# One pair of column blocks per feed-forward layer as seven block products in place of eight (Strassen's scheme)

## The reference

```python
def swiglu(x, w_gate, w_up, w_down):
    return (jax.nn.silu(x @ w_gate) * (x @ w_up)) @ w_down      # x 256x1024, w 1024x2816 and 2816x1024
```

## Time and profile before

| | |
|---|---|
| median of three runs | 1620.4 us (1619.58 to 1620.77) |
| profiled execution, span from first to last instruction | 1618.1 us |
| the median over that span | 2.3 us |
| TensorE matmul records | 7791 |
| weight and other data moved | 306.8 MB, mean 190 GB/s |

### The profile page before, as it was taken

How to read it: one execution, slowest core, us unless ns; L and a number is a source line. 1 busy time by engine, 2 the same in 40 slices (tenths; PEclk the granted TensorE clock), 3 DMA queues, 4 the chain that set the end, 5 groups by cost and what they waited for, 6 DMA issues and landing times.

```text
span 1618.1 us, 18458 instructions
## 1 busy us (share of the span) xinstructions
PE 1609.3 (99%) x7791; PEld 1342.0 (83%) x7791; DVE 957.4 (59%) x959; ACT 776.3 (48%) x815; POOL 78.7 (5%) x104
## 2 busy tenths in 40 slices
PE   9999999999999999999999999999999999999998
PEld 7888897788888888888988888888888998888886
DVE  6555466676554775455668545565446657685553
ACT  7444447655443764442656434354443436454340
POOL 0121000000000000001010000000000131000000
PEclk9999999999999999999999999999999999999999
DMA  9856474466654866563647546666555554576560
GB/s 319 231 179 208 157 240 140 163 198 219 192 187 131 276 205 185 159 221 98 237 158 253 182 156 211 204 201 188 161 206 182 196 178 148 182 241 188 162 216 26
DMA packets 222097, 306.77 MB, mean 190 GB/s; under 512 B 8896, under 2 KB 144320, under 8 KB 221888
## 3 DMA queue, kind: packets, MB, share of 16 engines
q1 hardware_dynamic: 217232, 290.29, 55.4%
q0 software_dynamic: 4416, 15.05, 2.9%
q10 hardware_dynamic: 368, 0.27, 0.1%
HBM read 304.52 MB, written 1.05 MB: 189 GB/s over the span
## 4 chain that ended last, share of the span: by engine, by line
PE 99%; DVE 0%; DMA 0%; SPq 0%; ACT 0%; issue 0%; DVEq 0%
PE bank L696 29%; PE bank L709 29%; PE bank L700 26%; PE bank L646 3%; PE bank L713 3%; PE bank L773 2%; PE bank L775 2%; PE bank L776 2%; PE bank L1117 0%; PE bank L907 0%; DMA raw<-in_ffn_w_up 0%; PE bank L926 0%; PE bank L916 0%; PE bank L1054 0%; PE bank L759 0%; PE bank L1136 0%
## 5 line engine op out<-in xcount | busy, mean ns | idle before, releaser
L1614 DVE TENSOR_TENSOR low<-raw,hiw 128x2048 fp32r<-128x2048 f32 (+2 forms) x296 | 631.4, 2143 | 382.9 <-ACT hiw L1229 381.9
L1229 ACT ACTIVATE hiw<-raw 128x2048 fp32r<-128x2048 f32 (+1 forms) x280 | 521.8, 1871 | 358.1 <-DMA raw<-in_ffn_w_out 87.9
L696 PE MATMUL bank<-hiw,xh 128*128 128x512 f32 x1404 | 384.9, 396 | 0.0
L709 PE MATMUL bank<-low,xh 128*128 128x512 f32 x1404 | 376.3, 390 | 0.0
L700 PE MATMUL bank<-hiw,xl 128*128 128x512 f32 x1232 | 330.1, 390 | 0.0
L709 PEld LDWEIGHTS bank<-low,xh 128*128 128x128 f32 x1404 | 263.2, 188 | 55.8 <-DVE low L1614 0.2
L696 PEld LDWEIGHTS bank<-hiw,xh 128*128 128x128 f32 x1404 | 257.1, 188 | 52.5 <-issue 2.8
L700 PEld LDWEIGHTS bank<-hiw,xl 128*128 128x128 f32 x1232 | 231.2, 188 | 49.6
L696 PE MATMUL bank<-hiw,th 128*128 128x512 f32 x524 | 143.7, 392 | 0.0
L700 PE MATMUL bank<-hiw,tl 128*128 128x512 f32 x524 | 142.2, 389 | 0.0
L709 PE MATMUL bank<-low,th 128*128 128x512 f32 x524 | 142.1, 389 | 0.0
(11 more groups left out here) (276 smaller groups left out, 1177.9 us busy)
## 6 DMA issues: line engine op xcount, KB each, us to landing
raw<-in_ffn_w_in SPq DMA_DIRECT2D x176, 512.0 KB, 4.9
raw<-in_ffn_w_out SPq DMA_DIRECT2D x40, 1024.0 KB, 5.0
raw<-in_ret_w_in SPq DMA_DIRECT2D x24, 1024.0 KB, 5.1
raw<-in_ffn_w_gate SPq DMA_DIRECT2D x42, 512.0 KB, 4.3
raw<-in_ffn_w_up SPq DMA_DIRECT2D x42, 512.0 KB, 5.3
raw<-in_ffn_w_down SPq DMA_DIRECT2D x20, 1024.0 KB, 5.1
raw<-in_w_in SPq DMA_DIRECT2D x16, 1024.0 KB, 5.7
raw<-in_gla_w_in SPq DMA_DIRECT2D x12, 1024.0 KB, 5.2
```

Source lines behind the costliest of these rows:

```text
L696: pe.matmul(o[:, :], tokens(0, k), whi[:, k, :], start=start and k == 0, stop=False, skip_group_check=True)
L709: ins = pe.matmul(o[:, :], tokens(0, k), wlo[:, k, :], start=False, stop=end, skip_group_check=True)
L1229: act.activation(hiw[s][:, 0:n], raw[s][:, 0:n], ACT.Copy).then_inc(hi.mark(i), 1)
L1614: dve.tensor_tensor(low[s][:, c0:c1], raw[s][:, c0:c1], hiw[s][:, c0:c1].bitcast(F32), ALU.subtract).then_inc(lo.mark(*what), 1)
```

## The change

In each feed-forward layer blocks 3 and 4 are computed together. With x11, x12 the first 128 tokens over rows 0 to 511 and 512 to 1023, x21, x22 the other 128, b11, b21 the weights of block 3 and b12, b22 those of block 4 for the same halves of the rows, the seven products are b11, t1, t2, b22, t3, b21, t4 (named by their weight operand): t1 = b12 - b11, t2 = b22 - t1, t4 = b21 - t2, t3 = b22 - b12. The token operands are x11, s0, s1, s3, s2, x12, x22 with s0 = x21 + x22, s1 = s0 - x11, s2 = x11 - x21, s3 = x12 - s1. Each product is one pass of 12 matmuls, alternately into banks 6 and 7, which the gate and up products didn't use. All sums are made in fp32 on DVE, and their results are split into high and low parts like any tile. Between the products stand whole tiles of the blocks 5 to 8, and the turns of the pair come later than in order:

```diff
+LOAD_LEAD, HIGH_LEAD = 6, 4
+FFN_PAIRS = (3,)
+FFN_STEPS = (
+    ("tile", 0, 0), ("tile", 0, 1), ("tile", 1, 0), ("tile", 1, 1), ("turn", 0),
+    ("token sums",),
+    ("tile", 2, 0), ("tile", 2, 1), ("turn", 1), ("blocks",),
+    ("product", 0, "b11"), ("tile", 5, 0),
+    ("product", 0, "t1"), ("tile", 5, 1), ("turn", 2),
+    ("product", 0, "t2"), ("tile", 6, 0),
+    ("product", 0, "b22"), ("tile", 6, 1), ("turn", 5), ("p",),
+    ("product", 0, "t3"), ("tile", 7, 0), ("turn", 4),
+    ("product", 0, "b21"), ("tile", 7, 1), ("turn", 6),
+    ("product", 0, "t4"), ("tile", 8, 0), ("tile", 8, 1), ("turn", 3), ("turn", 7),
+    ("tile", 9, 0), ("tile", 9, 1), ("turn", 8),
+    ("tile", 10, 0), ("tile", 10, 1), ("turn", 9))
```

PE's part, with what each product waits for:

```diff
+        def pe_product(pe, i, xh_of, xl_of, o, start):
+            whi, wlo = weight(i)
+            pe_hi(pe, i)
+            for k in range(4):
+                pe.matmul(o[:, :], xh_of(k), whi[:, k, :], start=start and k == 0, stop=False, skip_group_check=True)
...
+                elif m == "t1":
...
+                        pe.wait_ge(fn.sem, fn.of("sh", name))
+                        pe.wait_ge(vec.sem, vec.of("sl", name))
...
+                    pe_product(pe, grp[g].t1, *s_block(f, 0), bank[7], True)
+                elif m == "t2":
+                    pe.wait_ge(fn.sem, fn.of("u1", name, g))
+                    pe_product(pe, grp[g].t2, *s_block(f, 1), bank[6], False)
+                elif m == "b22":
+                    pe.wait_ge(fn.sem, fn.of("s5", name, g))
+                    pe_product(pe, grp[g].b22, *s_block(f, 3), bank[7], False)
+                elif m == "t3":
+                    pe.wait_ge(fn.sem, fn.of("u2", name, g))
+                    pe_product(pe, grp[g].t3, *s_block(f, 2), bank[6], False)
+                elif m == "b21":
+                    pe.wait_ge(vec.sem, vec.of("c12", name, g))
+                    pe_product(pe, grp[g].b21, *x_block(0, 1), bank[7], True)
+                else:
+                    pe.wait_ge(vec.sem, vec.of("c22", name, g))
+                    pe_product(pe, grp[g].t4, *x_block(1, 1), bank[6], False)
```

ACT copies the running sums u1, s5 and u2 out of PSUM, into memory of `xn` that is free meanwhile, and takes silu of the finished ones. DVE makes the weight sums in front of the lows, the token sums, and adds the copies to later products:

```diff
+        def dve_weight_sums(dve, i):
...
+            if m == "b11":
+                freed(dve, load_after[g.t1])
+                loaded(g.b11)
+                loaded(g.t3)
+                dve_sum(dve, g.t1, g.t3, g.b11)
...
+            elif m == "b22":
+                dve_sum(dve, g.t3, g.b22, g.t3)
...
+            dve.tensor_tensor(xs, xh[:, :, :].bitcast(F32), xl[:, :, :].bitcast(F32), ALU.add).then_inc(
+                vec.mark("xs", name), 1)
...
+            dve.tensor_tensor(sx[:, 0, :, :], a21, a22, ALU.add).then_inc(vec.mark("s", name, 0), 1)
...
+                if m == "b22":
+                    added(g, grp[g].b22, "u2", u2, bank[7], "c12")
+                    times(u2[:, 256:512], u2[:, 256:512], u2[:, 0:256], second, 0)
+                elif m == "t3":
+                    added(g, grp[g].t3, "s5", s5, bank[6], "c22")
+                    times(s5[:, 256:512], s5[:, 256:512], s5[:, 0:256], second, 1)
```

Weight memory is now given in single blocks of 128 x 2048, 14 at most (12 in f1 and f2), one for the raw and low part and one for the high part of a tile, each to the oldest, along an order of loads, highs and sums. The high part can wait for another tile than the load, so ACT has a wait of its own for it:

```diff
+            for i in range(first, end):
+                if tiles[i].pieces:
+                    events.append((load_key[i] - LOAD_LEAD, "load", i))
+                events.append((i - HIGH_LEAD, "high", i))
...
+                        load_key[grp.t3], load_key[grp.b22], load_key[grp.b21] = (
+                            grp.b11 + 0.5, grp.t1 - 0.1, grp.t2 - 0.1)
...
-            while j + 1 < NT and j < i + 5 and freed_by[j + 1] <= i - 2:
+            while j + 1 < NT and j < i + 5 and needed[j + 1] <= i - 2:
```

More of the change, by code:

```diff
@@ L98 @@
 Weight = namedtuple("Weight", "pieces k width")
-Ffn = namedtuple("Ffn", "name nx turned_raw th tl sg hh")
+Ffn = namedtuple("Ffn", "name nx turned_raw th tl sx sh sl sg hh")
+Group = namedtuple("Group", "first second b11 t1 t2 b22 t3 b21 t4")
 Edge = namedtuple("Edge", "n nx kind gains scale final early mid late")
@@ L235, in build @@
             rvl1 = sb("rvl1", [P, 2048], F32R, ar)
[L236 to L239, removed]
+        weight_block()
+        weight_block()
         U = []
@@ L387, in build @@
[L387 to L395, removed]
@@ L816, in pe_ffn @@
                 turn(0)
[L817 to L829, removed]
-                if j:
-                    turn(j - 1)
+                steps = FFN_STEPS[LEAD_STEPS:]
+            for step, *what in steps:
+                if step == "tile":
+                    tile(*what)
+                elif step == "turn":
+                    turn(*what)
+                elif step == "product":
+                    product(*what)
             T = (f.th, f.tl)
@@ L1588, in act_program @@
             act.wait_ge(tile_1.sem, tile_1.of("first"))
[L1589 removed]
+            act.activation(split[high_to[1]][:, 0:1024], whole[load_to[1]][:, 0:1024], ACT.Copy).then_inc(hi.mark(1, "first"), 1)
             act_turn_in(act, 0, 1)
@@ L1843, in dve_ffn @@
                 turn(0)
-            for j in range(0 if name == "f1" else 2, 11):
-                dve_lows(dve, 4 if name == "f1" and j == 0 else ahead(gu[2 * j + 1]))
-                mult(j, 0)
-                mult(j, 1)
-                if j:
-                    turn(j - 1)
-                if name == "f2" and j == 4:
+                steps = FFN_STEPS[LEAD_STEPS:]
+            for step, *what in steps:
+                if step == "tile":
+                    j, n = what
+                    if name == "f1" and j == 0:
+                        dve_lows(dve, 4)
+                    else:
+                        dve_lows(dve, ahead(spot[name, j, n]))
+                    if n:
+                        mult(j, 0)
+                        mult(j, 1)
+                elif step == "turn":
+                    turn(*what)
+                elif step == "token sums":
+                    dve_token_sums(dve, f)
+                elif step == "blocks":
+                    dve.wait_ge(fn.sem, fn.of("sh", name))
+                    dve.tensor_tensor(f.sl[:, :, :, :], f.sx[:, :, :, :], f.sh[:, :, :, :].bitcast(F32),
+                                      ALU.subtract).then_inc(vec.mark("sl", name), 1)
+                elif step == "product":
+                    dve_lows(dve, ahead(spot[(name, *what)]))
+                    product(*what)
+                elif step == "p" and name == "f2":
                     dve.wait_ge(fn.sem, fn.of("ph"))
```

382 lines of the change are left out of this document (291 added, 91 removed).

## The result

The changed kernel takes 1622.37 us (median of 20 runs, 1621.38 to 1624.62). The kernel before took 1620.24 us beside it (20 runs, 1619.58 to 1621.07). The ratio is 1.0014, 95% interval 1.0008 to 1.0021. So nothing was gained: the time rose by 2.1 us, which is within 0.2% of no change. The forecast was 1608.0 us, with a range of 1603.6 to 1616.0, and the time lies outside it.

A forecast was written before the change was run, and what follows sets the result against it. PE was taken as the bound, 99% of the chain. 16.3 - 4 x 0.9 - 0.3 = 12.4 us off the 1618.1 span gives 1605.7; with the median 2.3 above, 1608.0 us, range 1603.6 to 1616.0.

The forecast's parts named there:

- The price removed: PE, six feed-forward layers: 72 matmuls fewer of 7791, 2.72 us a layer, 16.3 us in all.
- The ledger of a0: Layer a0, turn of block 1 to turn of block 4: DVE needs 40.0 us, so PE waits 0.9 us.
- the four layers named: a0, a1, b0, b1: each waits 0.9 us at block 4's turn; f1 and f2 were forecast not to wait.
- the rivals that priced it higher: DVE's wide operations before block 4's turn: 2.29 us each, 1615 (chance 0.16); or 2.33 or more, up to 1641 (0.06).
- ACT's new wait: ACT's highs wait for a freed block, but `ahead` asks for none not free two tiles before; no cost counted.
- covered by 4 us: End of a0 and b0: one down tile loads late, 10.9 us for a way of 9.3, wanted 2.7 later still.
- if the clock of PE falls in a layer: Sign that the prediction is wrong: PE's clock falling within a layer; no size given.
- allowed 0.3 us: Layer f1: no wait at block 4's turn, but 0.3 us allowed for GpSimd's additions slowing about three lows.
- the margin in a0: Low of t1 in a0: DVE done at 609.5, PE wants it at 610.2.
- the four rivals: Whole kernel: full cover 1604.1 (chance 0.22), DVE later 1615 (0.16), slower 1641 (0.06), no gain 1620 (0.04).
- or other waits eat them exactly: Whole kernel, no place named: matmuls not removed, or their gain cancelled by other waits, 1620 us; chance 0.04.

The follow-up runs named there:

- both_fixes: Changed kernel with earlier-freed blocks for the early pieces at f2's and a1's edges, and block 4's turn moved behind product b21: 1605.52 us.
- wait_long: Kernel before, with ACT's high of b0's tile (1,0) at a1's edge made to wait for a late down-tile pass: 1626.45 us, ratio 1.0038.
- filler: Changed kernel with matmuls whose result nobody reads ahead of the x turn, 14 at f2's edge and 16 at a1's: 1618.59 us.
- edge_a1_fixed: Changed kernel with another block for b0's tile (1,0) alone (a1's edge), f2's edge left: 1617.19 us, ratio 0.998.
- turn4_later: Changed kernel with the turn of block 4 moved behind product b21 in all three queues: 1617.92 us, ratio 0.9985.
- alloc_only: Changed kernel with all feed-forward pairs as plain block products again, keeping only the new one-by-one block allocation: 1633.84 us, ratio 1.0083.
- edge_f2_fixed: Changed kernel with other blocks for the small stage's tiles alone (f2's edge), a1's edge left: 1617.17 us, ratio 0.9981.
- wait_short: Kernel before, with ACT's high of b0's tile (1,0) at a1's edge waiting for a pass 2.7 us earlier than in wait_long: 1622.23 us.

## Why the prediction was wrong

1. **The price removed was right.** 7719 matmuls; with the waits gone, both_fixes gains 14.9 us with 2.0 us of waits left, 16.9 against the forecast 16.3.

2. **The ledger of a0 was right, to 0.2 us.** DVE and PE of the kernel after, from the turn of block 1 to that of block 4:

```profile
602.24 0.60 PE L735 MATMUL bank<-ident,hh 128*128 128x128 f32 x4
...
605.31 2.29 DVE L2137 TENSOR_TENSOR sl<-sx,sh 128x2048 fp32r<-128x2048 f32 x1 [1.11 <-ACT sh L1564]
607.52 2.29 DVE L1821 TENSOR_TENSOR whole<-whole 128x2048 f32<-128x2048 f32 x1
609.72 4.49 DVE L1817 TENSOR_TENSOR split<-whole,split 128x2048 fp32r<-128x2048 f32 x2
...
645.01 0.42 DVE L2091 TENSOR_TENSOR xn<-xn 128x256 f32<-128x256 f32 x1 [0.48 <-ACT xn L1510]
645.49 0.66 PE L735 MATMUL bank<-ident,xn 128*128 128x128 f32 x4 [0.84 <-DVE xn L2091]
```

The low of the token sums starts 3.07 us after the turn of block 1, as forecast (602.82 - 599.75). From it to the end of block 4's second gate product DVE takes 645.43 - 605.31 = 40.1 us, forecast 40.0. The turn was due at 602.24 + 42.25 = 644.5 and came at 645.5. It waits in the four layers named and not in f2. A weight sum (607.52) lasts 2.29 us and takes 2.20 of the queue, to 609.72; the forecast had 2.205, and the rivals that priced it higher fall.

3. **The failed step is the one on ACT's new wait.** The prediction said: "ACT's highs now also wait for a block of their own to be freed, but `ahead` asks for none whose block isn't free two tiles before." The sentence holds for every high that `ahead` asks for. It isn't all of them: `act_edge` and `dve_edge` ask for one of the next stage's first tiles by name (`e.early[-1]`), past `ahead`, and there the norm stands behind it in both queues. I had costed the edges by the loads ("covered by 4 us"). I looked at when a transfer must be issued and not at when a block must be empty for ACT. wait_long shows this step alone to be worth 6.2 us at one edge. The two edges are 10.9 us of the 14.4 between forecast and result.

4. **The clock wasn't in the sum at all.** It stood only among the signs of failure ("if the clock of PE falls in a layer"). 3.8 us of the 10.9 are the clock's, by filler. This hangs on point 3: without the long waits the clock is 1.00 at both edges (both_fixes).

5. **f1 was taken too lightly.** It was allowed 0.3 us; it lost 2.0, 1.0 of them at the low of t1 (the margin in a0 was 0.7 us by the ledger) and 1.0 at the turn of block 4. The two waits are shown to be DVE's; why f1 is behind a0's ledger by that much, with GpSimd beside it and dearer gate products, was not taken apart. So it is with the 0.4 to 1.0 us at the attention's first tile.

6. **The range** ended 6.4 us too low. The nearest of the four rivals was the last, "or other waits eat them exactly", with a chance of 0.04. It named no place, and none of the others had an edge in it: the new block waits were costed at nothing in one sentence, with no price for the case that their cover is gone.

## What to carry to other kernels

Where a resource is split more finely (single blocks in place of pairs) every user gets a release of its own. List all who ask, not only the planner's regular ones: early work at a stage's edge is asked for by hand, and there the queue behind it holds the norm that everyone waits for. For each, write down which pass frees what it takes; tiles that are gone through twice are freed late.

A wait of the bounding engine has a second price if it is long: 1.4 us cost 2.0, 4.2 us cost 6.2. That price was larger by some 0.9 us in other traces with the same wait. When one can't be avoided, matmuls whose results nobody reads, put into it, buy the clock back.

When a change of many parts comes out even, take out the part that was meant to be neutral and run it alone. Here a single run gave +13.4 us for that part, against 16.3 us of matmuls saved.

## What the runs showed of the hardware

- PE standing still for 3.6 to 4.5 us went with a granted clock of 0.50. It cost 1.7 us of PE's work in six of nine cases read by the windows (both edges of the changed kernel, f2's in edge_a1_fixed and turn4_later, a1's in alloc_only and wait_long), and in three with waits of 4.2 to 4.5 us it cost 2.5 to 2.8 (a1's in edge_f2_fixed and turn4_later, f2's in alloc_only). Waits of 1.4 us and of 0.85 us left it at 1.00. Between 1.4 and 3.6 us nothing was tried.
- Waits moved by what was moved: 2.7 us earlier on ACT (wait_short against wait_long) gave 2.7 us less on PE (4.15 to 1.44), through ACT's high, DVE's low and the norm.
- The hundredth of the work that was removed (72 matmuls of 7791) came in full once its waits were gone, although DVE's busy share had gone from 59% to 68%. What counted were two block releases and a turn that was 0.85 us late, not the share.
